# Differential attention woven into its own projections, with the two softmaxes scaled on ScalarE and added on GpSimd

## What is computed

```python
kv = rms_norm(h, kv_norm) @ kv_w                      # k and v: 1024 columns each
proj = xn @ w_in                                      # q and gate: 1024 columns each
q, k = partial_rope(q), partial_rope(k)
lam = exp(sum(lq[0]*lq[1])) - exp(sum(lq[2]*lq[3])) + lam_init
s = einsum('bhcqd,bhckd->bhcqk', q, k); prob = softmax(causal(s))
attn = prob[:, :, 0] - lam * prob[:, :, 1]            # two softmaxes of a head combined
o = einsum('bhqk,bhkv->bhqv', attn, v)
o = rms_norm(o, subln_g, 1e-5) * (1 - lam_init)
y = (o * silu(gate)) @ w_out
```

## Time and profile before

| | |
|---|---|
| median of 3 runs | 1244.96 us (1242.57 to 1250.34) |
| the profiled execution | 1243.18 us, its span 1241.4 us |
| PE, PEld busy | 1075.8 us (87%), 895.2 us (72%) |
| DVE, ACT, POOL busy | 509.3 (41%), 527.2 (42%), 696.0 us (56%) |
| granted TensorE clock, mean | 0.925 of full |
| L394 matmuls on the chain that ended last | 21% of the span |

### The profile page before, as it was taken

The page is one execution under the profiler, slowest core; times in us unless marked ns, Lnnn a source line. Parts: engine busy times, 40 slices in busy tenths (PEclk is TensorE's granted clock), DMA queues, the critical chain, the costliest instruction groups (busy, mean ns, idle before and its releaser), DMA issues. The chain is left out here.

```text
span 1241.4 us, 19776 instructions
## 1 busy us (share of the span) xinstructions
PE 1075.8 (87%) x8448; PEld 895.2 (72%) x8448; DVE 509.3 (41%) x678; ACT 527.2 (42%) x797; POOL 696.0 (56%) x311
## 2 busy tenths in 40 slices
PE   5999999999788599999969995889759879967685
PEld 4788889899688489998834453889647658845564
DVE  1125274412374645311361445543582350047542
ACT  5447454445437464444321231212333564454252
POOL 6945489988643879888600034000675749970060
PEclk9999999999898799999979998999778979985698
DMA  9641455555454345655633431000036535530150
GB/s 368 233 146 39 153 177 189 191 189 186 137 169 137 100 161 190 191 188 187 214 117 111 152 117 53 4 4 4 19 119 216 162 97 199 187 101 1 46 167 34
DMA packets 45847, 169.36 MB, mean 136 GB/s; under 512 B 5088, under 2 KB 5344, under 8 KB 45440
## 3 DMA queue, kind: packets, MB, share of 16 engines
q1 hardware_dynamic: 43312, 159.06, 38.2%
q0 software_dynamic: 2448, 9.05, 2.2%
HBM read 167.03 MB, written 1.05 MB: 135 GB/s over the span
## 5 line engine op out<-in xcount | busy, mean ns | idle before, releaser
L671 POOL TENSOR_TENSOR ring_r<-ring,high_r 128x1024 fp32r<-128x1024 f32 x256 | 636.8, 2512 | 232.0 <-ACT high_r L801 231.2
L801 ACT CAST high_r<-ring 128x1024 fp32r<-128x1024 f32 x256 | 264.8, 1049 | 262.3 <-DMA ring<-w 262.0
L420 PE MATMUL psum<-x_high,high_r 128*128 128x256 f32 x640 | 182.3, 285 | 1.6 <-DVE x_low L281 1.6
L420 PE MATMUL psum<-x_low,high_r 128*128 128x256 f32 x640 | 181.2, 283 | 0.0
L420 PE MATMUL psum<-x_high,ring_r 128*128 128x256 f32 x640 | 181.2, 283 | 0.0
L394 PE MATMUL psum<-high_r,x_high 128*128 128x512 f32 x320 | 129.0, 403 | 9.8 <-DVE x_low L277 6.6
L394 PE MATMUL psum<-ring_r,x_high 128*128 128x512 f32 x320 | 126.9, 396 | 0.0
L394 PE MATMUL psum<-high_r,x_low 128*128 128x512 f32 x320 | 126.6, 396 | 0.0
L586 DVE TENSOR_TENSOR arena<-arena 128x512 f32<-128x512 f32 x32 | 46.4, 1449 | 192.2 <-ACT arena L562 192.1
L420 PEld LDWEIGHTS psum<-x_high,high_r 128*128 128x128 f32 x640 | 122.9, 192 | 2.9 <-issue 2.3
L420 PEld LDWEIGHTS psum<-x_low,high_r 128*128 128x128 f32 x640 | 122.8, 192 | 0.5
(11 more groups left out here) (313 smaller groups left out, 1743.0 us busy)
## 6 DMA issues: line engine op xcount, KB each, us to landing
ring<-w SPq DMA_DIRECT2D x292, 512.0 KB, 3.3
row<-rows POOLq DMA_DIRECT2D x14, 512.0 KB, 8.4
arena<-relt SPq DMA_DIRECT2D x2, 1536.0 KB, 14.6
h<-x SPq DMA_DIRECT2D x1, 1024.0 KB, 4.9
arena<-lora POOLq DMA_DIRECT2D x2, 512.0 KB, 6.6
out<-h SPq DMA_DIRECT2D x1, 1024.0 KB, 4.0
con<-consts SPq DMA_DIRECT2D x1, 529.0 KB, 5.0
arena<-pT POOLq DMA_DIRECT2D x2, 256.0 KB, 4.0
```

What stands on the lines that cost most here:

```text
L420: ins = nc.tensor.matmul(out, a, b, start=(k == 0 and q == 0), stop=(k == KT - 1 and q == 2))
L671: nc.gpsimd.tensor_tensor(low(m), raw(m), read(high(m)), ALU.subtract).then_inc(low_made, 1)
L801: nc.scalar.copy(high(m), raw(m)).then_inc(high_made, 1)
```

## The change

The 8 projection tiles are reordered to k0, q0, v0, k1, q1, v1, gate 0, gate 1 (0 and 1 are halves of the columns; the weights are laid out in that order). Three come first, with the transposes of the first halves of k and q. The other five are put into the loop, 20 pieces over 16 rounds as `FILL2` says, with the transposes of k1 in round 5 and of q1 in round 7. All four of those transposed pairs go through one PSUM bank, 3. The product with v of pair g stands in round 2g+5 (2g+6 from g=4), and it reuses banks 2 and 3 for both halves of the heads. The norm of the first four heads moves into rounds 12 and 13. Rope is done in four half parts. In the combination VectorE keeps only the reciprocal; ScalarE multiplies the second row of reciprocals by -lambda and scales both softmaxes (four instructions), and GpSimd adds them (`combine`), at fixed places between its lows.

```diff
-                bank_ = 4 + _b if _i in SPLIT_T else 3 if _i == T_K else 6 + _b % 2
+                bank_ = 4 + _b if _i in SPLIT_T else 3 if _i in (T_K, T_QB) else 6 + _b % 2
...
+        KVQG = [(kD, 0), (qD, 0), (vD, 0), (kD, 1), (qD, 1), (vD, 1), (gD, 0), (gD, 1)]
+        KVQG_BANK = [0, 2, 0, 2, 0, 0, 0, 0]
+        KVQG_X = [xTb2, xT2, xTb2, xTb2, xT2, xTb2, xT2, xT2]
+        FILL2 = [2, 1, 1, 2, 2, 2, 1, 1, 1, 1, 1, 1, 1, 1, 1, 1]
+        FILLED2 = [sum(FILL2[:hh]) for hh in range(HEADS + 1)]
+        TILE_AT2 = {2: 3, 4: 4, 7: 5, 11: 6, 15: 7}
+        PAIR_AT2 = {5: ((0, 0, 2), (1, 0, 3)), 7: ((2, 1, 2), (3, 1, 3))}
+        PV_AT2 = {2 * g + 5 + (g >= 4): g for g in range(8)}
...
+                a, c = ((kD, 0), (qD, 1), (kD, 3), (qD, 4))[i]
+                pool.wait_ge(kv_act, c + 1)
+                pool.wait_ge(kv_dve, c + 1)
...
+            def combine(g):
+
+                pool.wait_ge(b_scaled, g + 1)
+                b0, b1 = sd[:, (2 * g) % 4, :], sd[:, (2 * g + 1) % 4, :]
+                nc.gpsimd.tensor_tensor(b0, b0, b1, ALU.add).then_inc(comb_ready, 1)
...
+            for until, work, i in ((8, rope, 0), (12, rope, 1), (18, combine, 0), (20, rope, 2), (21, combine, 1), (23, rope, 3),
+                                   (25, combine, 2), (27, combine, 3), (29, combine, 4), (31, combine, 5), (32, gate_rows, 0),
+                                   (33, combine, 6), (35, combine, 7), (36, gate_rows, 1)):
+                low_until(4 * W_KVQG + until)
+                work(i)
...
+            for c in range(3):
+                split_for(W_KVQG + c)
+                kvqg_act(c)
+                if c == 2:
+                    evacuate_pair(act, T_KB, 0, kDT, 0)
+                    evacuate_pair(act, T_KB, 2, qDT, 0)
...
-                src = psum[:, 2 * g:2 * g + 2, :].rearrange("p b (h t d) -> p (b h) t d", h=2, t=NT)
+                src = psum[:, 2:4, :].rearrange("p b (h t d) -> p (b h) t d", h=2, t=NT)
...
-                split_until(min(4 * W_OUT_B + 6 + hh, 4 * W_OUT_B + 8))
-                if hh == 14:
+                split_until(4 * W_KVQG + 12 + FILLED2[min(hh, HEADS)] + (7 if hh < HEADS else 8))
+                if hh >= 2 and hh % 2 == 0:
+
...
+                    act.wait_ge(rd_ready, g + 1)
+                    if g == 0:
+                        act.wait_ge(lam_done, 1)
+                    r1 = rd[g % 2][:, 1, :]
+                    settle(nc.scalar.activation(r1, r1, ACT.Copy, scale=nlam))
+                    for c in range(2):
+                        buf = sd[:, (2 * g + c) % 4, :]
+                        for t, cut in ((1, slice(0, 256)), (0, slice(256, 384))):
+                            ins = nc.scalar.activation(buf[:, cut], buf[:, cut], ACT.Copy, scale=rd[g % 2][:, c, t:t + 1])
+                    ins.then_inc(b_scaled, 1)
+                if hh == 12:
                     heads_square(0)
+                if hh == 13:
+                    heads_root(0)
                 if hh < HEADS:
...
+                if hh in PAIR_AT2:
+                    i, which, b = PAIR_AT2[hh][0]
+                    evacuate_pair(act, T_QB, i, (kDT, qDT)[which], b)
+                if hh in TILE_AT2:
+                    kvqg_act(TILE_AT2[hh])
...
-            heads_root(0)
...
+            for c in range(3):
+                kvqg_dve(c)
+            evacuate_pair(dve, T_KB, 1, kDT, 1)
+            evacuate_pair(dve, T_KB, 3, qDT, 1)
...
+                nc.vector.tensor_tensor(dst, src, per_head, ALU.mult).then_inc(o_taken, 1)
+                dve.wait_ge(o_taken, g + 1)
+
+            def heads_gate(g):
+
+                hl = slice(g * HALF, (g + 1) * HALF)
+                dve.wait_ge(gate_gain, g + 1)
...
-                    settle(nc.vector.reciprocal(rd[g % 2], sums[:, 2 * g:2 * g + 2, :]))
-                    settle(nc.vector.tensor_scalar(rd[g % 2][:, 1, :], rd[g % 2][:, 1, :], nlam, None, ALU.mult))
-                    b0, b1 = sd[:, (2 * g) % 4, :], sd[:, (2 * g + 1) % 4, :]
-                    for t, cut in ((1, slice(0, 256)), (0, slice(256, 384))):
...
-                    ins.then_inc(comb_ready, 1)
-            heads_norm(0)
+                    if g >= 2:
+                        dve.wait_ge(comb_ready, g - 1)
+                    nc.vector.reciprocal(rd[g % 2], sums[:, 2 * g:2 * g + 2, :]).then_inc(rd_ready, 1)
+                if hh in PAIR_AT2:
+                    i, which, b = PAIR_AT2[hh][1]
+                    evacuate_pair(dve, T_QB, i, (kDT, qDT)[which], b)
+                if hh in TILE_AT2 and TILE_AT2[hh] < 6:
+                    kvqg_dve(TILE_AT2[hh])
+                if hh == 12:
+                    heads_var(0)
+                if hh == 13:
+                    heads_norm(0)
...
+            heads_gate(0)
             heads_var(1)
             heads_norm(1)
+            heads_gate(1)
...
+            for c in range(2):
+                for i in range(4):
+                    if c == 0:
+                        transposed(pe, T_H7)(i)
+                    kvqg_piece(c, i)
+            kvqg_out(1)
+            for i in range(4):
+                kvqg_piece(2, i)
+                if i == 1:
+                    pe.wait_ge(roped, 1)
+                    for b in range(2):
+                        pe_transpose_pair(pe, T_KB, b, kD, b)
             pe.wait_ge(roped, 2)
-            pe_transposes(pe, T_QB, qD)
-            evacuated(pe, T_QB)
-            pe.wait_ge(kv_act, 8)
-            for hh in range(HEADS + 4):
+            for b in range(2):
+                pe_transpose_pair(pe, T_KB, 2 + b, qD, b)
+            bank_out(pe, 4 * T_KB + 3)
...
+                for i, which, b in PAIR_AT2.get(hh, ()):
+
+                    kvqg_out(4 + which)
+                    pe.wait_ge(roped, 3 + which)
+                    pe_transpose_pair(pe, T_QB, i, (kD, qD)[which], b)
+                if hh < HEADS:
+                    for n in range(FILLED2[hh], FILLED2[hh + 1]):
+                        if n % 4 == 0:
+
+                            kvqg_out((2, 3, 5, 6, 7)[n // 4])
+                        kvqg_piece(3 + n // 4, n % 4)
+                if hh == 5:
+                    kvqg_out(4)
+                if hh == 7:
+                    bank_out(pe, 4 * T_QB + 3)
+                if hh == 14:
+                    kvqg_out(6)
+                    pe.wait_ge(o_taken, 1)
+                if hh in PV_AT2:
...
+                    o = psum[:, 2 + g % 4 // 2, :].rearrange("p (h t d) -> p h t d", t=NT, d=P)[:, g % 2]
...
+            kvqg_out(8)
+            pe_linear(pe, W_OUT_B, 2, xT2, lambda pe, c: pe.wait_ge(o_taken, 2) if c == 1 else None, transposed(pe, T_OB))
...
+    kv_w, qg_w = f("kv_w_2"), f("b_w_in_2")[0]
+    for wm, c in ((kv_w, 0), (qg_w, 0), (kv_w, 2), (kv_w, 1), (qg_w, 1), (kv_w, 3), (qg_w, 2), (qg_w, 3)):
+        cols_tile(wm, c)
```

More of the change, by code:

```diff
@@ L490, in build @@
         kDT, qDT, oD, oD2 = view(4 * S, KT, SEQ), view(5 * S, KT, SEQ), view(6 * S, NT, D), view(7 * S, NT, D)
-        rt = [view(8 * S + 256 * i, NT, 16, 8) for i in range(4)]
+        rt = [view(8 * S + 128 * i, NT, 8, 8) for i in range(4)]
         sd = view(9 * S, 4, 384)
@@ L738, in _, with pool_settle, rope @@
             pool.wait_ge(con_landed, 16)
[L740 to L747, removed]
+            cosb = C("cos").rearrange("p (t f) -> p t f", t=NT).unsqueeze(2).broadcast_to([P, NT, 8, 8])
+            sinb = C("sin").rearrange("p (t f) -> p t f", t=NT).unsqueeze(2).broadcast_to([P, NT, 8, 8])
+            made_steps = [4]
+            def pool_settle(ins):
+                made_steps[0] += 1
+                ins.then_inc(pool_step, 1)
+                pool.wait_ge(pool_step, made_steps[0])
+            def rope(i):
+                a, c = ((kD, 0), (qD, 1), (kD, 3), (qD, 4))[i]
+                pool.wait_ge(kv_act, c + 1)
+                pool.wait_ge(kv_dve, c + 1)
+                v = a[:, :, (i // 2) * HALF:(i // 2 + 1) * HALF].rearrange("p t (s d) -> p t s d", d=64)
                 x1, x2 = v[:, :, :, 0:8], v[:, :, :, 8:16]
@@ L750, in _ @@
                     ins = nc.gpsimd.tensor_tensor(rt[d], s0, s1, ALU.mult)
[L751 to L753 removed]
+                pool_settle(ins)
                 nc.gpsimd.tensor_tensor(x1, rt[0], rt[1], ALU.subtract)
@@ L1036, in _, with kvqg_act @@
             act.wait_ge(rstd_ready, 9)
[L1037 to L1051, removed]
+            def kvqg_act(c):
+                dst, j = KVQG[c]
+                used(act, W_KVQG + c)
+                hl, bank = slice(j * HALF, (j + 1) * HALF), KVQG_BANK[c]
+                if c < 6:
+                    ins = nc.scalar.activation(dst[:, 0, hl], psum[:, bank, :], ACT.Copy, scale=rstd[:, 16:17])
+                else:
+                    for t in range(NT):
+                        ins = nc.scalar.activation(dst[:, t, hl], psum[:, bank + t, :], ACT.Silu, scale=rstd[:, 16 + t:17 + t])
+                ins.then_inc(kv_act, 1)
+            for c in range(3):
[4 more added lines that the diff above has]
```

(11 more changed lines are left out.)

64 lines of the change are left out of this document (27 added, 37 removed).

## The result

The changed kernel takes 1231.89 us (median of 6, 1228.11 to 1237.32) against 1244.58 us for the kernel before beside it (median of 6): ratio 0.9908, interval 0.9886 to 0.9929. That is 0.9% less, and the interval takes in the 1% that the prediction had put as its bound. Its profiled execution took 1231.78 us, span 1230.0 us, against 1243.18 and 1241.4.

A forecast was written before the change was run, and what follows sets the result against it. It took a chain through four engines to pace the head loop while TensorE waits. First score 1048.4, rounds 59.8, last rounds 38.0 and tail 8.4 end the stage at 1154.6; 13.7 less gives 1229.5 profiled, 1230 median, range 1219 to 1243.

The forecast's parts named there:

- first score: Start of the stage: third tile evacuated from 1044.24, plus 1.0 for two transposed pairs and 3.1 for queued evacuations, giving 1048.4.
- rounds 0 to 9: Woven loop: TensorE's rounds priced from the first attention at 53.9 us, plus 5.9 of bank waits, 59.8 in all.
- the waits for bank 3: Rounds 5 and 7: a transposed pair waits until ACT evacuates the one before, 3.2 and 2.7 us, 5.9 together.
- a wait for bank 0 in round 12: Round 12: one wait more for bank 0, half a us, taking the gain from 14.2 to 13.7 us.
- (e): Rival in the rounds: waits in rounds 5 and 7 keep TensorE's clock low, pieces at half rate, 19 us: 1248; chance 0.06.
- Cost 0: POOL's queue in the rounds: sums hold back the lows behind them, but 3.7 us of cover make it free.
- ACT's list: Last rounds: from round 11 ACT has more work than TensorE, 23.0 us after 9.8, ending the last scaling at 32.8.
- Rival (a): Last rounds: ACT's queue does not bind at the end, last sum at 27.1 instead of 33.9, 6.8 less: 1223; chance 0.15.
- Rival (b): ACT from round 11 on: each of five table loads costs another 1.28, list grows by 6.4: 1236; chance 0.05.
- (c): Rival in rounds 3 to 5: POOL's lows come late for the pieces, 6.5 us lost: 1236; chance 0.15.
- (d): Rival in the loop: TensorE and heads take turns, nothing hidden, 1.35 more per head, +15.5 in all: 1259; chance 0.09.
- The share for the port: Tail: VectorE's small `tensor_scalar` and gate product can each wait 0 to 2.3 for POOL's lows, together taken as 0.9.

## Why the prediction was right, step by step

It forecast 1230 in the median, and 1231.9 was measured; 1229.5 in the profile, and 1231.78. I had given 0.56 to a time below 1232.5, and 1231.9 lies just below it; against the kernel before as run beside it that is 0.9%. The forecast stood 1.2% below the shown median, so the bound of 1% was well inside the error of the forecast. In the stage, relative to its first matmul:

| step | predicted us | measured us |
|---|---|---|
| first score | +39.1 | +37.1 |
| rounds 0 to 9 | 59.8 | 61.0 |
| of it, the waits for bank 3 | 3.2 + 2.7 | 2.77 + 2.40 |
| from round 10 (1109.96) to the end of the last scaling | 32.8 | 33.0 |
| to the last transposes | 33.9 | 34.1 |
| to the square | 38.0 | 37.6 |
| from the square to the output projection | 8.4 | 8.8 |
| a wait for bank 0 in round 12 | 0.5 | none listed |
| the whole stage | 145.8 | 144.5 |

**First score.** From the third tile's evacuation 3.20 passed, predicted 3.1. The 2.0 came before it, and they are the clock. In the kernel before, the first ten matmuls of the stage stand 0.43 apart and reach the eleventh after 4.35 us (1009.31 to 1013.66). In this profile they stand 0.23 apart, after the same transposes and the same gap (1.06, there 1.11), and reach it after 2.39. The run of the same kernel again had the low clock there: its 120 matmuls took 29.63 instead of 27.49, and its first score came at +39.2, where 39.1 was predicted. So the term was right, and the total of 144.5 has 2.0 of luck in it: run again, the stage took 146.6 (1008.40 to 1155.02), 0.8 more than predicted.

**The rounds.** The busy part was priced right: 61.0 less 5.17 of waits and 1.9 of slow matmuls is 53.9, the number predicted from the first attention's intervals. The step that was left out of the sum is the clock behind the bank waits. I had it as a rival only, (e), for a third of the pieces; behind the second bank wait it came for one piece, granted clock 0.58, 1.9 us.

**The combination.** Costs of 1.7 (ACT) and 0.95 (POOL) were 1.8 and 0.95. "Cost 0" in the rounds held: doubling the sum cost 1.0, all of it at the last one. What I argued but left out of the sum is the credit: kept on VectorE in this loop, it costs 7.8 more in the median, 6.8 in the stretch. The sum counts TensorE's work only and needs VectorE to be in time; nothing in it says that the old combination would not have been. The rule of the Trainium skill that the prediction weighed against the change ("Perfetto Trace Analysis", Optimizing Scalar/DVE Operations: moving work between VectorE and GpSimd might not help) came out the other way, since the operations that waited for lows went to ScalarE, or became GpSimd's own. In the old loop the move did not help, but there the rows show a longer chain for each head and POOL's order, not the port.

**ACT's list.** Rival (a) is out: ACT was busy 23.32 of the last 23.60 us, and taking 2.5 and one cast from the list took 2.7 from the stretch. I took 23.0 for the part behind round 11's Silus, and it took 23.5 (1119.41 to 1142.95). The prediction's terms for it add up to 22.9, not to the 23.9 written there; the 23.0 that it took is right. Rival (b) is out: loads of 1.28 are followed by their activation 0.01 to 0.02 later. (c) is out: no gap of PE in the rounds was released by a low. The half us for one more wait for bank 0 has no gap in the timeline either; ACT's list sets the pace in that round. (d) is out in this loop, and its price per head was measured in the old one.

**The tail.** The share for the port was 0.9; L1567 took 1.14 (0.17 alone) and L1584 1.59 (1.23), 1.3 more together. The prediction's own terms give 8.5, not 8.4.

**Outside the stage.** I had assumed no difference there. The profile has +2.56 ahead and +1.1 behind. The code is the same. The 2.56 is scatter: the same kernel run again started the stage at 1008.40, 0.91 earlier than the kernel before, and the versions of the experiments started it between 1006.17 and 1014.81. The 1.1 is 1.5 more in the last 96 matmuls of the kernel and 0.4 less ahead of them: they took 24.87 us against 23.36, with 13 intervals of 0.43 between them in place of 5, the lower clock again (24.79 when run again). What decides how many stays open. So the profiled time was 2.3 above the forecast, +2.56 and +1.1 outside the stage less 1.3 inside, and these terms partly cancel by luck.

## What to carry to other kernels

Moving one operation off a loaded engine is worth what it removes from the path, and that depends on what else TensorE has in its order: the same new combination costs 9.9 us where TensorE waits for each head and saves some 7 where pieces lie between and VectorE works beside GpSimd's lows. When work is woven into a loop, look for a resource that is used twice in one round (here one PSUM bank for two pairs): spreading it was worth 5.4 us, for a change of order alone. And after each fix read the in-order queues again: ACT's list, then POOL's order, then a collision of VectorE and POOL were late in turn, and the last one gave back all that was won. And compare the clock at the edges of a stage before its total is read: here 2.0 of 15.0 us were the clock.

## What the runs showed of the hardware

- VectorE's `tensor_scalar` and its operations with two SBUF inputs were held up by GpSimd's lows, each instruction anew: two took 4.67 and 4.81 beside lows of 2.35. Small ones were too: 128x2 took 1.93 instead of 0.23, 128x8 1.14 instead of 0.17. It goes both ways: two lows took 5.64 beside a gate product of 1.66, where they take 4.65 to 4.77.
- TensorE's clock fell to the lower level (matmuls of 512 columns 0.43 apart) behind a gap of 2.40 us, for about 3.5 us, but not behind the gap of 2.77 us in round 5 of the same profile, and not behind gaps of 1.14 and 0.72. The four other profiles with these two gaps show the same. At the start of the stage, behind a gap of 1.06, the first ten matmuls of the same code ran at the lower level when the kernel was run again and at the full one in the first profile. These rows alone do not say what tells the cases apart.
- A table load took 1.28 us, and the next activation started 0.01 to 0.02 behind it in all five of the loop's last rounds (ScalarE in the changed kernel). The one in the tail at 1148.57 was followed at 1151.01, when VectorE had its input ready.
